# Sums of the conditioning products at the ends of two feed-forwards: four PSUM banks, and transposes with reductions for the column sums

## The reference, cut to what matters

```python
mod = jnp.split(jax.nn.silu(c) @ ada_w[l] + ada_b[l], N_MOD, axis=-1)
modc = jnp.split(jax.nn.silu(c_ctx) @ ada_w[l] + ada_b[l], N_MOD, axis=-1)
sh1, sc1, g1, sh2, sc2, g2 = [m[:, None, :] for m in mod]
u = jnp.concatenate([_layernorm(xc) * (1.0 + sc1c) + sh1c, _layernorm(x) * (1.0 + sc1) + sh1], axis=1)
x = _layernorm(DN_ALPHA * x + g1 * mix[:, n_ctx:], ln1_w[l], ln1_b[l])
h = _layernorm(x) * (1.0 + sc2) + sh2
x = _layernorm(DN_ALPHA * x + g2 * f, ln2_w[l], ln2_b[l])
```

## Time and profile before

| | us |
|---|---|
| median of three runs | 2011.38 |
| lowest and highest | 2009.25, 2022.72 |
| the profiled execution, own time | 2009.26 |
| its span, first to last instruction | 2007.5 |

### The profile page before, as it was taken

How to read it: one execution, slowest core, us unless ns; L and a number is a source line. 1 busy time by engine, 2 the same in 40 slices (tenths; PEclk the granted TensorE clock), 3 DMA queues, 4 the chain that set the end, 5 groups by cost and what they waited for, 6 DMA issues and landing times.

```text
span 2007.5 us, 33575 instructions
## 1 busy us (share of the span) xinstructions
PE 1866.7 (93%) x14234; PEld 1336.9 (67%) x14234; DVE 978.3 (49%) x1456; ACT 640.9 (32%) x1002; POOL 336.2 (17%) x317
## 2 busy tenths in 40 slices
PE   7988999899998899989999989979999999999981
PEld 6878998889988899858575579874333333333330
DVE  5746776555564677732545754663322222222116
ACT  5544333444444533321234332422111112111110
POOL 2101000000000111000010034402233333333413
PEclk9989999999999999978999989979999999999986
DMA  8535775778743888512011200075999999999995
GB/s 280 190 106 186 244 243 196 253 290 305 252 139 116 291 307 311 192 42 84 1 43 45 89 19 4 20 300 201 398 373 366 377 368 368 371 376 379 378 399 200
DMA packets 199700, 456.76 MB, mean 228 GB/s; under 512 B 32982, under 2 KB 154326, under 8 KB 170000
## 3 DMA queue, kind: packets, MB, share of 16 engines
q1 hardware_dynamic: 157104, 377.18, 51.1%
q0 software_dynamic: 35712, 58.00, 8.2%
q10 hardware_dynamic: 6752, 19.67, 2.7%
HBM read 549.91 MB, written 52.43 MB: 300 GB/s over the span
## 4 chain that ended last, share of the span: by engine, by line
PE 86%; DVE 7%; DMA 2%; ACT 2%; issue 2%; POOL 1%; ACTq 0%; POOLq 0%; DVEq 0%
PE psum L350 33%; PE psum L3526 16%; PE psum L3510 8%; PE psum L1610 7%; PE psum L1617 2%; PE psum L3452 2%; PE psum L2666 2%; PE psum L2650 1%; DVE w_lo L411 1%; DMA mem<-in_exp_w_dram,mem 1%; PE psum L3539 1%; ACT w_hi L406 1%; PE psum L570 1%; PE psum L3209 1%; DMA y_rows<-mem 1%
## 5 line engine op out<-in xcount | busy, mean ns | idle before, releaser
L411 DVE TENSOR_TENSOR w_lo<-mem,w_hi 128x2048 fp32r<-128x2048 f32 x122 | 279.0, 2290 | 195.1 <-ACT w_hi L406 190.7
L350 PE MATMUL psum<-x_hi,w_hi 128*128 128x256 f32 x1216 | 349.6, 288 | 4.4 <-DVE x_lo L557 4.4
L3526 PE MATMUL psum<-mem 128*64 128x512 f32 x1536 | 344.8, 602 | 6.7 <-DMA mem<-in_exp_w_dram,mem 6.7
L350 PE MATMUL psum<-x_hi,w_lo 128*128 128x256 f32 x1216 | 344.6, 283 | 0.0
L350 PE MATMUL psum<-x_lo,w_hi 128*128 128x256 f32 x1216 | 343.7, 283 | 0.0
L406 ACT ACTIVATE w_hi<-mem 128x2048 fp32r<-128x2048 f32 x122 | 233.8, 1918 | 196.9 <-PE psum L350 192.0
L3526 PEld LDWEIGHTS psum<-mem 128*64 128x64 f32 x1536 | 107.0, 138 | 205.7 <-issue 195.5
L350 PEld LDWEIGHTS psum<-x_hi,w_hi 128*128 128x128 f32 x1216 | 234.0, 192 | 10.1 <-DVE w_lo L411 4.8
L350 PEld LDWEIGHTS psum<-x_lo,w_hi 128*128 128x128 f32 x1216 | 237.4, 195 | 0.7
L350 PEld LDWEIGHTS psum<-x_hi,w_lo 128*128 128x128 f32 x1216 | 236.5, 194 | 0.0
L3510 PE MATMUL psum<-mem 128*64 128x512 f32 x768 | 175.3, 598 | 1.2 <-DVE mem L3612 1.2
(11 more groups left out here) (508 smaller groups left out, 2837.5 us busy)
## 6 DMA issues: line engine op xcount, KB each, us to landing
mem<-in_exp_w_dram SPq DMA_DIRECT2D x192, 1024.0 KB, 10.4
mem<-in_dil_w_qkv_dram SPq DMA_DIRECT2D x36, 1024.0 KB, 5.8
mem<-in_ada_w_dram POOLq DMA_DIRECT2D x48, 512.0 KB, 6.5
mem<-in_ffn_w_gate_dram SPq DMA_DIRECT2D x22, 1024.0 KB, 5.9
mem<-in_ffn_w_up_dram SPq DMA_DIRECT2D x22, 1024.0 KB, 6.8
mem<-in_ffn_w_down_dram SPq DMA_DIRECT2D x22, 1024.0 KB, 4.8
mem<-in_w_in_dram SPq DMA_DIRECT2D x13, 1024.0 KB, 5.5
mem<-in_na_w_qkv_dram SPq DMA_DIRECT2D x12, 1024.0 KB, 8.4
```

Source lines behind the costliest of these rows:

```text
L350: ins = pe.matmul(out, lhs[a], rhs[b], start=start and k == 0, stop=stop and k == 2, **kw)
L411: dve.tensor_tensor(w_lo[n % SLOTS][:, 0, :], ring[:, n % SLOTS, :], w_hi_f[n % HI][:, 0, :], ALU.subtract).then_inc(S("w_split"), 1)
L3526: ins = pe.matmul(psum[r, up, :].rearrange("p (a n) -> p a n", a=2), xg[:, b % 2, c, x * P + 64 * e:x * P + 64 * e + 64], w_up[s][e][:, :, ...
```

## The change

Both places use four banks (2, 3, 0, 1 in this order) in place of two. As banks 0 and 1 hold the last up product, both functions wait first for `ex_hid` of the last tile. In `mod_pe` a group waits for the reduction four before it, no longer two. In `mod2_pe` the four row products wait for nothing among themselves. The column sums of j = 3 and 4 become four groups of four transposes, each into the bank whose row sum VectorE has added up, and four reductions along the free axis on VectorE, followed by two small operations that add the bias (and one, for the scale, j = 4). `mod2_rows` counts to nine in place of five, and `ctx_turn_pe` waits for that.

```diff
--- before.py
+++ after.py
@@ -451,7 +451,7 @@
         k = norm_n["pe"]
         norm_n["pe"] += 1
         pe.wait_ge(S("norm_rows"), NT * (k + 1))
-        pe.wait_ge(*at("mod2_rows", len(MOD2_ROWS) + 1))
+        pe.wait_ge(*at("mod2_rows", MOD2_DONE))
         turn_pe(pe, ctx_tok, "norm_turned")
 
     def ctx_out_act(act):
@@ -1457,20 +1457,23 @@
 
     MOD_SUMS = [(j, v, half) for j in MOD_1 for v in range(2) for half in range(2)]
 
+    SUM_BANK = (2, 3, 0, 1)
+
     def mod_pe(pe):
         pe.wait_ge(S("mod_used"), N_ROWS1)
+        pe.wait_ge(S("ex_hid"), N_FF)
         for g, (j, v, half) in enumerate(MOD_SUMS):
-            if g >= 2:
-                pe.wait_ge(*at("mod_done", g - 1))
+            if g >= 4:
+                pe.wait_ge(*at("mod_done", g - 3))
             for c in range(4):
-                ins = pe.transpose(bank(2 + g % 2, P, c * P), mod1_acc[:, j, v, 4 * half + c::KC], ident)
+                ins = pe.transpose(bank(SUM_BANK[g % 4], P, c * P), mod1_acc[:, j, v, 4 * half + c::KC], ident)
             ins.then_inc(S("mod_T"), 1)
 
     def mod_dve(dve):
 
         for g, (j, v, half) in enumerate(MOD_SUMS):
             dve.wait_ge(S("mod_T"), g + 1)
-            dve.tensor_reduce(modT[:, j, v, 4 * half:4 * half + 4], bank(2 + g % 2).rearrange("p (c n) -> p c n", c=4), X,
+            dve.tensor_reduce(modT[:, j, v, 4 * half:4 * half + 4], bank(SUM_BANK[g % 4]).rearrange("p (c n) -> p c n", c=4), X,
                               ALU.add).then_inc(S("mod_done"), 1)
         dve.wait_ge(*at("mod_done", len(MOD_SUMS)))
         for j in MOD_1:
@@ -1507,29 +1510,36 @@
 
     MOD2_ROWS = [(j, g, h) for j, g in ((2, g1_b), (5, g2_b)) for h in range(2)]
 
+    MOD2_COLS = [(j, half) for j in (3, 4) for half in range(2)]
+    MOD2_DONE = len(MOD2_ROWS) + len(MOD2_COLS) + 1
+
     def mod2_pe(pe):
         pe.wait_ge(S("mod_used"), N_ROWS1 + N_ROWS)
+        pe.wait_ge(S("ex_hid"), 2 * N_FF)
         for n, (j, g, h) in enumerate(MOD2_ROWS):
-            if n >= 2:
-                pe.wait_ge(*at("mod2_rows", n - 1))
-            pe.matmul(bank(2 + h), C("ones"), mod_acc[j][:, 512 * h:512 * h + 512], start=True, stop=True
+            pe.matmul(bank(SUM_BANK[n]), C("ones"), mod_acc[j][:, 512 * h:512 * h + 512], start=True, stop=True
                       ).then_inc(S("mod_sums"), 1)
-        pe.wait_ge(*at("mod2_rows", 3))
-        for m, j in enumerate((3, 4)):
-            for c in range(KC):
-                ins = pe.matmul(bank(2, 1, 8 * m + c), mod_acc[j][:, c::KC], C("ones")[:, 0:1], start=True, stop=True)
-        ins.then_inc(S("mod_sums"), 1)
+        for n, (j, half) in enumerate(MOD2_COLS):
+            pe.wait_ge(*at("mod2_rows", n + 1))
+            for c in range(4):
+                ins = pe.transpose(bank(SUM_BANK[n], P, c * P), mod_acc[j][:, 4 * half + c::KC], ident)
+            ins.then_inc(S("mod_sums"), 1)
 
     def mod2_dve(dve):
         dve.wait_ge(S("mod_in"), 16 * 8)
         for n, (j, g, h) in enumerate(MOD2_ROWS):
             dve.wait_ge(S("mod_sums"), n + 1)
             gh = g[:, 512 * h:512 * h + 512]
-            dve.tensor_tensor(gh, gh, bank(2 + h), ALU.add).then_inc(S("mod2_rows"), 1)
-        dve.wait_ge(S("mod_sums"), 5)
-        dve.tensor_tensor(modT[:, 3, 0, :], ada_cols[:, 3, :], bank(2, KC), ALU.add)
-        dve.scalar_tensor_tensor(modT[:, 4, 0, :], bank(2, KC, 8), 1.0, ada_cols[:, 4, :], ALU.add, ALU.add
-                                 ).then_inc(S("mod2_rows"), 1)
+            dve.tensor_tensor(gh, gh, bank(SUM_BANK[n]), ALU.add).then_inc(S("mod2_rows"), 1)
+        for n, (j, half) in enumerate(MOD2_COLS):
+            dve.wait_ge(S("mod_sums"), len(MOD2_ROWS) + n + 1)
+            dve.tensor_reduce(modT[:, j, 0, 4 * half:4 * half + 4], bank(SUM_BANK[n]).rearrange("p (c n) -> p c n", c=4), X,
+                              ALU.add).then_inc(S("mod2_rows"), 1)
+        dve.wait_ge(*at("mod2_rows", MOD2_DONE - 1))
+        for j in (3, 4):
+            ins = dve.scalar_tensor_tensor(modT[:, j, 0, :], modT[:, j, 0, :], float(j - 3), ada_cols[:, j, :], ALU.add,
+                                           ALU.add)
+        ins.then_inc(S("mod2_rows"), 1)
 
 
     top[0] = stage_top
```

## The result

The changed kernel takes 1997.8 us (median of seven runs, 1992.48 to 2009.05) against 2009.47 us (seven runs of the kernel before, 2004.99 to 2022.72). The ratio is 0.9935 with a 95% interval of 0.9910 to 0.9961: between 7.8 and 18 us less. The forecast was 9.3 us less, 2001.0, and no change that clears 1%; 9.3 lies inside that interval too, so whole times alone do not tell the measured gain from the forecast one.

What follows compares the result with a forecast made beforehand. TensorE was taken to bound the kernel (busy 93% of the span, 86% of the chain), with VectorE leading behind the first place's sums. The terms 0.9 + 6.0 + 2.4 = 9.3 us gave 2001.0 us, range 1995 to 2010.

Steps and rivals of the forecast that it cites:

- The new waits for ex_hid cost nothing: Both places: the last up product's readers finish before TensorE needs banks 0 and 1; cover 1.1 us at the second; cost 0.
- First place, 0.9 us: End of the first feed-forward: VectorE's eight reductions run without gaps on four banks; 0.9 us gained, bounds 0.6 to 1.8.
- Row sums, 0.4 us: Second feed-forward's end: four row products without waits among themselves take 3.4 us; this alone gives some 0.4 us.
- column sums, 6.0 in all: Second place: sixteen transposes replace 32 one-column passes; down product starts near 852.4 in place of 858.45, 6.0 us earlier.
- Clock, 2.4 us: Second place: first half of the down product at full clock, 3.06 us in place of 5.49; 2.4 us, bounds 0 to 2.4.
- the clock falls all the same: Rival, second place: transposes do not hold the clock; gain 6.9 us, time 2003.4; chance 0.12.
- VectorE's slack, 2.6 us: Second place: VectorE finishes reductions and small additions 2.6 us before L624 can go, so the new reductions cost nothing.
- VectorE leads at the second place: Rival: slower reductions, or the residual hanging on them, shrink the gain of 8.4 there to some 5; time 2004.5; chance 0.06.
- The sum, 9.3 us: Whole kernel: first place 0.9, second-place sums 6.0 and clock 2.4 add to 9.3 us; forecast time 2001.0.
- I let all of it pass to the end: Behind both places: every wait moves with the work, weight loads included, so the whole 9.3 us reaches the end.
- shorter restarts: Rival: restarts at half clock shorten, one from 9.2 to 5.6 us and others alike; 4 to 8 us more, 1995; chance 0.08.
- longer restarts: Rival, every restart in the second block: 20% more half clock, 19 us of time, result about 2021; chance 0.07.

Runs made afterwards that it cites:

- The row sums alone: Kernel before, with only the second place's row sums spread over four banks and the one-column products kept; 2009.62 us, one run.
- the wide products: Kernel before, with its sixteen one-column products at the second place made 128 columns wide; 2010.10 us, one run.
- four times the transposes: Changed kernel with each of the sixteen column transposes at the second place done four times (64 in place of 16); 2004.52 us, one run.
- the tripled reductions: Changed kernel with each of the four column reductions at the second place done three times (twelve in place of four); 2001.02 us, one run.
- the pad of 1.3 us: Changed kernel with two extra VectorE writes of 512 columns behind the first place's sums; 2000.54 us (seven runs), ratio 0.9940.
- pad: Changed kernel with ten extra VectorE writes of 512 columns behind the residual of the second feed-forward; 2004.51 us, one run.
- the split moved ahead: Changed kernel with one of the two w_lo splits behind the first place moved ahead of its eight reductions; 1995.74 us (four runs), ratio 0.9942.

## Why the prediction was right, point by point

- *The new waits for ex_hid cost nothing*: at the second place L756 was over at 844.36, 1.1 us before the row sums began (845.49), the cover that was worked out; at the first place it was 3.4 us. The kernel without the waits was not run.
- *First place, 0.9 us*: 0.9 in all six profiles with four banks and no other edit there. VectorE leads; TensorE's 1.8 us (down product at 3.00 in place of 4.80) are not seen at the end.
- *Row sums, 0.4 us, and column sums, 6.0 in all*: 5.14 us from the first row sum to the down product in place of 11.41, so 6.27. The row sums alone gave 0.56. The gain was put a little too small because the transposes' price was put too high, at 0.12 us each; sixteen took 1.79 on the chain, 0.11 each.
- *Clock, 2.4 us*: 2.43, shown by the wide products, which also show the cause that the prediction only implied: it took the fall to go with the column products. The rival "the clock falls all the same" is refuted, with four times the transposes.
- *VectorE's slack, 2.6 us*: 2.75, and the tripled reductions paid only what went beyond. The rival "VectorE leads at the second place" is refuted.
- *The sum, 9.3 us*: the parts measured 9.6. The time lies in the range, 3.2 us below the forecast (1997.8 against 2001.0), which the medians do not resolve: their interval is 7.8 to 18 us. Between the two profiles the step that did not hold is "I let all of it pass to the end": 11.5 us of span are gone, more than the parts. The rival "shorter restarts" named the mechanism and the size (4 to 8 us more, 1995), but I took it as a spread without a sign, at 0.08. In these two stages it has one: 2.3 us in the second layer, which the first place's 0.9 us set off and the pad of 1.3 us took back, and 2.4 us in the mixed product, which came with every early arrival and went with each of the three late ones of the changed kernel (tripled reductions, pad, four times the transposes). That they reach the whole time is not shown: the first pad took back 2.3 us in its stage and nothing that the medians show, and the split moved ahead came 3.4 us early without a gain. The rival "longer restarts" did not occur.

The +1.1 us behind the mixed product and the +1.6 us ahead of the first place are of the size by which the two profiles of the changed kernel differ there (1.2 and 2.0 us); what makes them differ was not looked into.

## What to carry to other kernels

A sum over partitions by one-column products took 0.24 us a pass here, as much as with 128 columns, and left TensorE at half clock for what followed; transposes into a bank and reductions on an engine that was idle were 7.2 us cheaper for 16 such columns, 2.4 of them the clock's. Where a kernel has restarts at half clock, a small gain ahead of one may be worth more or less than its own size: read in the windows when the clock came back relative to the first instruction, in several profiles, before calling the difference chance, or a gain. And ask of a freed bank only where the other engine's wait is on the chain: the banks gave 1.5 us, the kind of instruction 7.2.

## What the runs showed of the hardware

- The clock's first return and the program keep nearly in step: it rose within 159 to 163 us in every profile, and the first reduction began 181.9 to 182.8 us after that rise in all of thirteen, though its own start varies from 342.66 to 344.65. Behind this the restarts of one kernel do not always come out alike: of the two profiles of the changed kernel one has 3.4 us of half clock near 413 and the other none, and the runs of the kernel before differ in mean granted clock, from 0.948 to 0.959, and in time, from 2004.9 to 2022.7 us.
- At the second restart the outcome has two sides. With L570 up to 202.0 us after the clock's last rise before it (between 658 and 668) the clock was back 2.8 to 4.2 us after L570 began and the mixed product took 14.1 us (six profiles); with L570 202.5 us or later it was back 7.8 to 9.5 us after, and the product took 15.7 to 16.6 (seven profiles). This is what thirteen profiles show, not a threshold: the starts between 202.0 and 202.5 were not tried, nor what decides between them.
- fp32 passes with 128 x 128 weights loaded anew came 0.24 us apart with 1 column and with 128, at 1.2 GHz and at 2.4; fp32 transposes 0.11 us apart, at a held full clock.
